# Two transformer blocks on one core: earlier banks, norm sums in parts, a row spread by repeated columns, operands ahead of weights

## What is computed

```python
# block 1
h = rms_norm(x, g_mix_pre); proj = h @ w_in        # q, k, v of two attentions, and 8 forget logits
log_f = log_sigmoid(f_logit + b_fgate)              # cumulated over tokens: the decay of fox attention
x = x + rms_norm(concat(rms_norm(fox), rms_norm(chunked)) @ w_out, g_mix_post)
x = x + rms_norm(memory_cross_attention(rms_norm(x, g_mem_pre), m), g_mem_post)
x = x + rms_norm(swiglu(rms_norm(x, g_ffn_pre)), g_ffn_post)
# block 2
h = rms_norm(x, mixer_norm)                         # "mixer_2": rstd = 1 / sqrt(mean(x * x) + eps)
q, k = rms_norm over each head of (h @ attn_w_in);  v = h @ attn_w_in
x = x + dilated_window_attention(q, k, v) @ attn_w_out
x = x + conv_ffn(rms_norm(x, ffn_norm))             # "ffn_2", then the product called conv_up
```

## Time and profile before

| | |
|---|---|
| median of 3 runs | 1579.5 us (1578.61 to 1580.58) |
| the profiled execution | 1580.17 us, of which the span of the trace is 1578.4 us |
| PE busy | 1539.4 us, 98% of the span |
| DVE, ACT, POOL busy | 884.3, 594.2, 243.5 us |
| mean granted clock of PE | 0.993 |

### The profile page before, as it was taken

How to read it: one execution, slowest core, us unless ns; L and a number is a source line. 1 busy time by engine, 2 the same in 40 slices (tenths; PEclk the granted TensorE clock), 3 DMA queues, 4 the chain that set the end, 5 groups by cost and what they waited for, 6 DMA issues and landing times.

```text
span 1578.4 us, 21219 instructions
## 1 busy us (share of the span) xinstructions
PE 1539.4 (98%) x7428; PEld 1269.6 (80%) x7428; DVE 884.3 (56%) x1239; ACT 594.2 (38%) x889; POOL 243.5 (15%) x273
## 2 busy tenths in 40 slices
PE   9999999999999999999999999999999999999998
PEld 6787777886887788888888678888997788888887
DVE  6434777437452743343332786846877766767323
ACT  6123433544244422222322642334764433334222
POOL 0200000015002300000000455554441000000000
PEclk9999999999999999999999999999999999999999
DMA  5532000431203233323323122323002233332331
GB/s 165 187 96 92 1 1 26 161 107 54 81 12 96 75 94 98 106 81 106 106 80 107 54 80 83 105 81 99 9 1 80 80 106 91 95 106 80 107 106 54
DMA packets 152799, 132.07 MB, mean 84 GB/s; under 512 B 6300, under 2 KB 137628, under 8 KB 152740
## 3 DMA queue, kind: packets, MB, share of 16 engines
q1 hardware_dynamic: 150836, 128.11, 26.5%
q0 software_dynamic: 848, 3.17, 0.6%
q10 hardware_dynamic: 1056, 0.00, 0.0%
HBM read 129.15 MB, written 2.12 MB: 83 GB/s over the span
## 4 chain that ended last, share of the span: by engine, by line
PE 87%; DVE 6%; POOL 2%; ACT 2%; issue 1%; DMA 0%; DVEq 0%; SPq 0%; ACTq 0%; POOLq 0%
PE ps L1764 24%; PE ps L1766 24%; PE ps L1765 24%; PE ps L2021 3%; PE ps L433 2%; POOL x_t L739 2%; PE ps L2150 1%; DVE work L1254 1%; PE ps L466 1%; PE ps L568 1%; PE ps L2009 1%; DVE a_lo L1275 1%; PE ps L2137 1%; DVE work L1353 1%; PE ps L1952 1%
## 5 line engine op out<-in xcount | busy, mean ns | idle before, releaser
L1764 PE MATMUL ps<-a_hi,w_hi 128*128 128x512 f32 (+2 forms) x1656 | 646.3, 390 | 15.0 <-DVE a_lo L1275 7.4
L1766 PE MATMUL ps<-a_hi,w_lo 128*128 128x512 f32 (+2 forms) x1656 | 641.0, 387 | 0.0
L1765 PE MATMUL ps<-a_lo,w_hi 128*128 128x512 f32 (+2 forms) x1656 | 640.6, 387 | 0.0
L1764 PEld LDWEIGHTS ps<-a_hi,w_hi 128*128 128x128 f32 (+1 forms) x1656 | 312.3, 189 | 88.2 <-issue 13.4
L1766 PEld LDWEIGHTS ps<-a_hi,w_lo 128*128 128x128 f32 (+1 forms) x1656 | 312.1, 188 | 64.0
L1765 PEld LDWEIGHTS ps<-a_lo,w_hi 128*128 128x128 f32 (+1 forms) x1656 | 312.5, 189 | 62.5 <-issue 0.7
L817 ACT ACTIVATE w_hi<-raw 128x2048 fp32r<-128x2048 f32 x118 | 225.8, 1913 | 348.6 <-PE ps L1766 346.8
L1227 DVE TENSOR_TENSOR w_lo<-raw,w_hi 128x2048 fp32r<-128x2048 f32 x94 | 216.1, 2298 | 247.0 <-ACT w_hi L817 246.7
L744 POOL TENSOR_TENSOR w_lo<-raw,w_hi 128x2048 fp32r<-128x2048 f32 x24 | 110.6, 4608 | 451.3 <-ACT w_hi L817 451.3
L1621 DVE TENSOR_TENSOR arena<-ps,rstd 128x512 f32<-128x512 f32 x88 | 60.1, 689 | 166.3 <-PE ps L1766 160.0
L1691 DVE RECIPROCAL rstd<-std 128x512 f32<-128x512 f32 x24 | 80.5, 3353 | 26.3 <-ACT std L1141 26.3
(11 more groups left out here) (235 smaller groups left out, 1562.3 us busy)
## 6 DMA issues: line engine op xcount, KB each, us to landing
raw<-in_w_gate_up SPq DMA_DIRECT2D x44, 512.0 KB, 4.6
raw<-in_ffn_w_up SPq DMA_DIRECT2D x44, 512.0 KB, 4.6
raw<-in_attn_w_in SPq DMA_DIRECT2D x36, 512.0 KB, 4.3
raw<-in_w_in SPq DMA_DIRECT2D x24, 512.0 KB, 4.8
raw<-in_w_down SPq DMA_DIRECT2D x22, 512.0 KB, 4.2
raw<-in_ffn_w_down SPq DMA_DIRECT2D x22, 512.0 KB, 4.2
raw<-in_w_mem_kv SPq DMA_DIRECT2D x16, 512.0 KB, 4.1
raw<-in_w_out SPq DMA_DIRECT2D x8, 512.0 KB, 4.4
```

The costliest lines, as they stand in the source:

```text
L1764: pe.matmul(dst, s_hi, m_hi, start=start, stop=False, skip_group_check=across)
L1765: pe.matmul(dst, s_hi, m_lo, start=False, stop=False, skip_group_check=across)
L1766: return pe.matmul(dst, s_lo, m_hi, start=False, stop=stop, skip_group_check=across)
```

## The change

Four edits are spread over the queues.

1. DVE takes the first two tiles of fox_qk out of PSUM in the middle of the gate chain, ahead of a weight split.
2. The eight squares of mixer_2 are summed in parts: DVE reduces tiles 0 to 3 (`half_sum`), POOL adds tiles 4 and 5 and tiles 6 and 7, and DVE adds both results. PE waits for the third of these steps. For that, POOL's memset of `q_pad_2` goes behind all its work for dil_in, and the low part of the first squares behind the split of chunk 2. The squares of ffn_2 are reduced in two parts by DVE, the first one between the third and the fourth residual add of dil_out's last chunk.
3. The row of mixer_2 is spread by four products of a repeated column with the identity, so the product of identity and column on DVE goes.
4. ACT makes `a_hi` of tiles 4 and 5 of ffn_2 ahead of the weights and the squares of tiles 4 to 7 at the end, and `enter` is left out before conv_up.

```diff
@@ POOL
             add_residual("ffn_post", y_ffn)
-            pool.memset(q_pad_2, 0.0).then_inc(pad_2_cleared, 1)
+            for k in (4, 6):
+                pool.wait_ge(norms["mixer_2"].sq, k + 2)
+                pool.tensor_tensor(y_ffn[:, k, :], y_ffn[:, k, :], y_ffn[:, k + 1, :], ALU.add)\
+                    .then_inc(norms["mixer_2"].value, 1)
...
                 if ch.first_of_gemm:
-                    squares_split(0)
                     return
                 split_lo(ch)
                 if ch.second_of_gemm:
-                    squares_split(1)
+                    squares_split(0), squares_split(1)
...
             dil_groups(pool, dil_chunk)
+            pool.memset(q_pad_2, 0.0).then_inc(pad_2_cleared, 1)
@@ ACT
             over_chunks(act, G["dil_out"], wide, peel=1)
+            act.wait_ge(tile_done, G["dil_out"].signal_end)
+            only_hi("ffn_2", x_block2, (4, 5))
             split_hi(Chunk(G["conv_up"], 0, 2, 0))
-            gained_hi("ffn_2", x_block2, range(4, KT))
+            only_hi("ffn_2", x_block2, (6, 7))
+            for k in range(4, KT):
+                squared("ffn_2", k)
@@ DVE
             def invert_pre(name):
...
+                if name == "mixer_2":
+                    half_sum(name)
+                    for k in (4, 6):
+                        dve.wait_ge(norm.value, 1 if k == 4 else 2)
+                        dve.wait_ge(norm.added, k // 2 - 1)
+                        dve.tensor_tensor(square_sum, part_sum if k == 4 else square_sum, of[:, k, :], ALU.add)\
+                           .then_inc(norm.added, 1)
+                    return
+                dve.wait_ge(norm.sq, KT)
+                if name == "ffn_2":
+                    dve.wait_ge(norm.added, 1)
+                    dve.tensor_reduce(square_sum, nine_squares[:, 4:9, :].rearrange("p k n -> p n k"), axis=AX.X, op=ALU.add)\
+                       .then_inc(norm.added, 1)
...
+            def half_sum(name):
+                dve.wait_ge(norms[name].sq, 4)
+                dve.tensor_reduce(part_sum, x_squares[name][:, 0:4, :].rearrange("p k n -> p n k"), axis=AX.X, op=ALU.add)\
                    .then_inc(norms[name].added, 1)
...
             def invert_mixer(norm):
...
-                dve.tensor_tensor(diagonal.rearrange("p (b n) -> p b n", b=4),
-                                  ident[:, :].rearrange("p (b n) -> p b n", b=1).to_broadcast([128, 4, 128]),
...
             dve.reciprocal(w, u_).then_inc(gate_step, 1)
+            for j in range(2):
+                query_key(Chunk(G["fox_qk"], 0, 2, 0), j, 0)
             split_lo(Chunk(G["fox_qk"], 0, 2, 1))
...
                     dve.sem_inc(freed["dve"], 1)
+                    if ch.c == 1 and j == 2:
+                        half_sum("ffn_2")
@@ PE
+            def spread_mixer(norm):
+                pe.wait_ge(norm.inverse, 1)
+                for b in range(4):
+                    last = pe.matmul(ps[:, 5, b * 128:(b + 1) * 128], tok_eps_mean[:, b:b + 1].to_broadcast([128, 128]),
+                                     ident[:, :], start=True, stop=True, skip_group_check=True)
+                last.then_inc(norm.spread, 1)
...
-                            pe.wait_ge(norms["mixer_2"].added, 1)
+                            pe.wait_ge(norms["mixer_2"].added, 3)
...
-            feature_major("conv_up", "dil_out", ready=norms["ffn_2"].ready, tail=1)
+            feature_major("conv_up", "", ready=norms["ffn_2"].ready, tail=1)
```

More of the change, by code:

```diff
@@ L326, in two_blocks_kernel @@
         norms = {n: Norm(n, ("value",)) for n in ("mix_post", "mem_post", "ffn_post")}
-        norms.update({n: Norm(n, ("rstd", "hi", "ready")) for n in ("mem_pre", "ffn_pre", "mixer_2", "ffn_2")})
+        norms.update({n: Norm(n, ("rstd", "hi", "ready")) for n in ("mem_pre", "ffn_pre", "ffn_2")})
+        norms["mixer_2"] = Norm("mixer_2", ("value", "rstd", "hi", "ready"))
         class Turn:
@@ L844, in gained_hi, with only_hi, squared @@
                     act.activation(x_squares[name][:, k, :], x_t[:, k, :], ACT.Square).then_inc(norm.sq, 1)
+            def only_hi(name, ready, tiles):
+                for k in tiles:
+                    act.wait_ge(ready, k + 1)
+                    act.activation(a_hi[:, k, :], x_t[:, k, :], ACT.Identity, scale=vcol(name, k)).then_inc(norms[name].hi, 1)
+            def squared(name, k):
+                act.activation(x_squares[name][:, k, :], x_t[:, k, :], ACT.Square).then_inc(norms[name].sq, 1)
             def rstd_out(name, gemm):
@@ L1251, in invert_pre @@
             def invert_pre(name):
[L1253 to L1254 removed]
+                norm, of = norms[name], x_squares[name]
+                if name == "mixer_2":
[11 more added lines that the diff above has]
+                       .then_inc(norm.added, 1)
+                else:
+                    dve.tensor_reduce(square_sum, of.rearrange("p k n -> p n k"), axis=AX.X, op=ALU.add)\
+                       .then_inc(norm.added, 1)
+                invert(norm)
+            def half_sum(name):
+                dve.wait_ge(norms[name].sq, 4)
+                dve.tensor_reduce(part_sum, x_squares[name][:, 0:4, :].rearrange("p k n -> p n k"), axis=AX.X, op=ALU.add)\
                    .then_inc(norms[name].added, 1)
[L1256 to L1257 removed]
             def invert_mixer(norm):
@@ L1490, in _, with query_key @@
             split_lo(Chunk(G["fox_qk"], 0, 2, 0))
+            def query_key(ch, j, first):
+                dve.wait_ge(tile_done, ch.before + (j + 1))
+                dve.tensor_tensor(flat(ch.c * (2 * S) + (QK_1 + (first + j) * S), S), ps[:, (ch.o * 2 + j) % 4, :],
+                                  rstd[:, :], ALU.mult).then_inc(freed["dve"], 1)
             z, e, u_, ln = (work[0:8, a * S:(a + 1) * S] for a in range(4))
@@ L1523, in body @@
                 def body(ch):
-                    if not (split_ahead and (ch.first_of_gemm or ch.second_of_gemm)):
+                    if split_ahead and ch.first_of_gemm:
+                        return
+                    if not (split_ahead and ch.second_of_gemm):
                         split_lo(ch)
                     for j in range(2):
-                        dve.wait_ge(tile_done, ch.before + (j + 1))
-                        dve.tensor_tensor(flat(ch.c * (2 * S) + (QK_1 + (first + j) * S), S), ps[:, (ch.o * 2 + j) % 4, :],
-                                          rstd[:, :], ALU.mult).then_inc(freed["dve"], 1)
+                        query_key(ch, j, first)
                 over_chunks(dve, G[name], body, peel=int(split_ahead))
@@ L2205, in dil_tiles @@
                     if ch.second_of_gemm and j == 0:
-                        spread(norms["mixer_2"])
+                        spread_mixer(norms["mixer_2"])
                         head_mean(0, 0)
```

8 lines of the change are left out of this document (3 added, 5 removed).

## The result

| | before | changed |
|---|---|---|
| median | 1579.59 us (5 runs, 1578.61 to 1580.58) | 1587.54 us (5 runs, 1587.09 to 1589.03) |
| the profiled execution | 1580.17 us, span 1578.4 | 1589.03 us, span 1587.2 |
| PE busy | 1539.4 us | 1545.2 us |
| mean granted clock of PE | 0.993 | 0.990 |

The ratio is 1.0053, with a 95% interval of 1.0041 to 1.0066: the change makes the kernel slower by 8.4 us (6.5 to 10.4). The forecast was 1583.8 with a range of 1576.5 to 1587.5. The sign was right, the size was half of what came, and the time lies just above the range. The profiled execution is the longest of the five, 1.5 us over their median.

What follows compares the result with a forecast made beforehand. PE, busy in 98% of the span, was taken as the bound. Terms -3.5 + 1.3 + 1.3 + 3.0 + 1.1 + 0.1 + 1.0 = +4.3 us gave 1584.5, for the median 1583.8 us; range 1576.5 to 1587.5.

Steps and rivals of the forecast that it cites:

- Gate chain, -3.5: Gate chain near 43 us: PE's 1.86 us wait goes, and the half clock behind it, 1.6 us: -3.5 us.
- The price of the strided `tensor_reduce`: mixer_2 half sum: strided elements cost 1.8 ns each, so 2048 elements take 3.86 us.
- I take DVE first by a hair.: mixer_2, about 904.8: DVE's first add precedes POOL's split, the second add waits until 910.5; spread 913.1 against 911.80, +1.3 us.
- rival 3: mixer_2: POOL takes the port first at 904.8, the sum comes 1.2 us later; +5.5, 1585.0 us; chance 0.15.
- Of the 1.6 us a part falls into the wait: +1.3.: mixer_2: a PE wait of 3.7 us should halve the clock too, costing +1.3 us.
- The sum for the spread, 910.5 + 2.54: mixer_2: time of the spread, 910.5 + (911.80 - 1.49 - 907.77), given as 913.1 against 911.80 before: +1.3 us.
- The memset, +3.0 and +1.1: First scores of dilated attention: the late q_pad_2 memset makes PE wait 3.0 us, with halved clock +1.1 us.
- conv_up, +0.1 and +1.0: conv_up, sixth operand tile: one wait of 2.1 us replaces two short ones, +0.1 us; clock behind it +1.0 us.
- Rival 1: mixer_2 and conv_up: POOL does not hold up DVE's adds and `a_lo`; -2.9 us, 1576.6; chance 0.17.
- rival 4: Dilated attention: the memset is hidden, ACT's wait not reaching PE; +0.2 us, 1579.7; chance 0.08.
- Rival 2: Whole kernel: the clock does not fall behind the new waits; +0.9 us, 1580.4; chance 0.15.

Runs made afterwards that it cites:

- the one with the filled wait: Changed kernel with 18 extra, unread TensorE products ahead of PE's wait for the mixer_2 sum of squares: 1584.52 us, ratio 1.0036.
- the kernel with POOL behind both adds: Changed kernel with POOL's split of dil_in's third chunk held until DVE's two adds of squares are done: 1581.50 us, ratio 1.0017.
- the tie decided for DVE: Changed kernel with POOL's split of dil_in's third chunk held until DVE's first add of squares is done: 1587.14 us, ratio 1.0047.
- POOL held at conv_up: Changed kernel, memset in idle time, POOL after both mixer_2 adds (low part, then split), conv_up split held until DVE's last operand low part: 1571.10 us, 0.9951.

## Why the prediction was half right

- **Gate chain, -3.5.** The steps are right (tiles out at 37.7 for 37.3, split done at 39.9 for 39.5, both late by the 0.4 us by which the reciprocal started later than before; no wait, no half clock there). Alone it gave -2.8 (-4.1 to -1.4), so the size is right within what can be measured.
- **The price of the strided `tensor_reduce`** is right: 3.90 us for 2048 elements, 3.86 predicted by 1.8 ns each, where the Trainium skill's basic rate (VectorE: DVE Perf Modes, the perf-mode tier table) would have given about 2.3, an estimate. POOL's second add of squares ran beside its start (to 900.18), and it was not held up: with POOL idle the same reduction took 3.88.
- **"I take DVE first by a hair."** In the profiled execution it was POOL, by 0.06 us: rival 3's order, with its wait of 4.9 us. Four profiled executions left the order open. POOL was first in the changed kernel and in the one with the filled wait, whose openings ran at full clock; DVE was first with mixer_2 alone and with the memset in idle time, where 6.8 us of half clock lay in the opening. So the step hung on something that no sum can know, and it was worth 0.9 us of waiting, not 1.2. The mechanism, that one of the two waits out the other's whole instruction and is served at the next boundary, is shown by the runs that move POOL. The Trainium skill (SBUF — State Buffer, on the shared port pair) states it as an exclusive lock for a DVE instruction with two SBUF inputs and a GpSimd one that reads SBUF; the 5.04 and 0.69 us of one and the same add agree.
- **"Of the 1.6 us a part falls into the wait: +1.3."** This is the term that failed. The mechanism was right, half clock behind the wait, but its size was taken from the one behind the gate's 1.86 us, 3.41 us long with 7 products lost, less a part. Behind the four unfilled waits for this sum (4.89, 4.03, 3.25 and 3.23 us) it lasted 6.8 us each time, and it cost 2.7 to 2.8. With 0.9 for the order that makes mixer_2 about 2.6 + 1.4 + 0.9 = 4.9, an estimate; measured +5.5 (3.6 to 7.4). (The sum for the spread, 910.5 + 2.54, is 913.0 and not 913.1, which changes nothing.)
- **The memset, +3.0 and +1.1.** Right: the wait is 2.94 us, the part alone costs +3.9, and taking it away gives 4.3. The clock term held because the fall behind this wait was mostly the short one: 1.3 us for 3.4 us of half clock. In the changed kernel's own trace it was the long one, 2.5 us.
- **conv_up, +0.1 and +1.0.** The size in all is right, 1.4 (0.0 to 2.8) for 1.1, with waits of +0.57 for +0.1. POOL served between two low parts fits the rows. That +1.0 of clock comes on top is not shown, as said above; if it doesn't, the agreement is partly luck.
- **Rival 1** (DVE's adds not held up) and **rival 4** (hidden memset) are refuted, by the adds of 5.04 us and by the memset alone. **Rival 2** (no fall behind the new waits) does not hold at mixer_2, where the filled wait gains 2.7 us; behind single waits of single executions it does (the 2.34 us of the kernel with POOL behind both adds; in the kernel with the filled wait also the 2.94 at the scores and the 2.21 at conv_up).

In all: forecast +4.3, measured +8.4. Of the 4.1 us between, mixer_2 has 2.9, the gate 0.7, conv_up 0.3, and the memset gives back 0.2; the 0.4 that are left are within the margins. Each of the four has a margin of over 1 us, and only that of mixer_2 (1.9) is clear of zero. Could it have been seen? Every fall in the trace of before lasts 3.4 us, so no row there showed one of 6.8. But the wait in my own sum was 3.7 us, twice the 1.86 whose fall I priced it by, and I gave it no upper bound.

## What to carry to other kernels

Before two-operand work is moved to POOL or brought forward on DVE, look for what the other engine starts in the same microsecond: a POOL instruction of 4.6 us makes a DVE add of 0.69 us take 5 us, and putting POOL behind the short ones gave 5.7 us at one place (1.0053 to 1.0017) and 3.6 at another (0.9974 to 0.9951). A cheap instruction is hidden only where it stands: the memset of 1.8 us was free in idle time and cost 3.9 us at the head of the attention. Price a wait of PE with the clock behind it, and where it is longer than any wait whose fall the trace shows, leave room for a longer fall; where a long wait can't be removed, products thrown away in it are worth a trial.

## What was not expected of the hardware

**The clock's falls are not tied to a place.** All 14 profiled executions have the same wait of 1.36 or 1.37 us in the memory attention, at 152 to 157 us. In nine of them, before and the gate part alone among them, full clock follows; in four 3.4 us of half clock (the memset alone, mixer_2 alone, the tie decided for DVE, POOL held at conv_up); in the changed kernel 6.8 us. In the 77 executions of the kernel before that ran beside the experiments, the mean granted clock ran from 0.992 to 0.997 and the time from 1577.5 to 1582.8 us, and they go together: the 22 at 0.997 have a mean of 1577.7 us, the 17 at 0.993 one of 1580.4, some 0.7 us per 0.001. So a sum made against one profiled execution carries an error of about 2 us (an estimate from this spread) that no working can remove, and a time read as the difference of two traces does too. The Trainium skill (TensorE: Matmul & The Clock Gate, Part 1) says that the observation runs free of the kernel's start and runs of one kernel differ by it; these executions agree.

**A slow stretch and a wait trade.** With DVE's first add ahead of POOL, PE's wait at the sum is 4.03 us where the opening ran at full clock, and 3.25 and 3.23 where 6.8 us of half clock lay in it. A shorter wait in a trace is then no gain.

**Filling a wait speeds the kernel up**: 18 useless products, 4.24 us of PE, gave 2.7 us in the times and 2.8 in the trace.
